# Late modulation of a diffusion layer: four products in four column strips of TensorE

## The reference, cut to what matters

```python
mod = silu(c) @ w_mod + b_mod          # two vectors c; w_mod is 1024 x 6144
shift1, scale1, gate1, shift2, scale2, gate2 = six parts of 1024
h  = x * (1.0 + scale1) + shift1
x  = layer_norm(ALPHA * x + gate1 * mix(h), ln1_g, ln1_b)
h2 = x * (1.0 + scale2) + shift2
x  = layer_norm(ALPHA * x + gate2 * peer(h2), ln2_g, ln2_b)
```

## Time and profile before

| | |
|---|---|
| median of three runs | 3380.88 us |
| the profiled execution | 3382.47 us, of which the span is 3380.5 us |
| TensorE busy, share of the span | 3271.4 us, 97% |
| mean granted clock of TensorE | 0.989 |
| late modulation, L852 from first to last start | 365.4 to 412.5 us |
| first output projection, L895 | from 430.1 us |
| `experts` block, L1673 | from 1220.0 us |

### The profile page before, as it was taken

One profiled execution on the slowest core, in us unless ns is written; L12 is line 12 of the kernel. 1 busy time (PEld: TensorE's weight loads), 2 busy tenths in 40 slices (PEclk: granted clock), 3 DMA queues, 4 the chain that ended last, 5 costly groups with the idle time before them and its releaser, 6 DMA issues.

```text
span 3380.5 us, 46340 instructions
## 1 busy us (share of the span) xinstructions
PE 3271.4 (97%) x17054; PEld 2748.4 (81%) x17054; DVE 2591.1 (77%) x5319; ACT 1237.8 (37%) x2289; POOL 1563.1 (46%) x969
## 2 busy tenths in 40 slices
PE   8999999999998879999999999999999999999997
PEld 3566367787887669998999999998999999999996
DVE  0232137888877879998999888889899998888866
ACT  1232233333332853333333333333333433333333
POOL 1100000688866238888888888432233232222201
PEclk9999999999999989999999999999999999999998
DMA  9600525666667589999999999999998999998943
GB/s 394 256 21 19 226 113 187 188 172 179 168 189 206 203 307 350 344 355 340 350 355 352 367 351 362 382 358 340 361 369 344 367 369 352 357 350 343 352 161 122
DMA packets 290754, 952.91 MB, mean 282 GB/s; under 512 B 92901, under 2 KB 146277, under 8 KB 231784
## 3 DMA queue, kind: packets, MB, share of 16 engines
q1 hardware_dynamic: 154314, 513.36, 41.1%
q0 software_dynamic: 135936, 436.53, 37.6%
q10 hardware_dynamic: 288, 0.16, 0.0%
HBM read 888.70 MB, written 61.24 MB: 281 GB/s over the span
## 4 chain that ended last, share of the span: by engine, by line
PE 52%; DVE 8%; DMA 3%; issue 1%; ACT 1%; SPq 0%; DVEq 0%; ACTq 0%
PE bank L1673 26%; PE bank L1687 26%; DMA work<-in_u 2%; DVE ring L1800 2%; DVE acc L1817 2%; DVE uL L1986 1%; DVE vL L1981 1%; DVE ga L2013 1%; DVE cL L1978 0%; ACT vR L1752 0%; DVE slots L1922 0%; ACT uR L1760 0%; DMA work<-x_scratch 0%; DVE st L1946 0%; DVE slots L1943 0%
## 5 line engine op out<-in xcount | busy, mean ns | idle before, releaser
L1634 POOL DMA_INDIRECT ring<-in_uv,slots x384 | 582.8, 1518 | 794.2 <-DVE carry L1817 684.8
L163 POOL DMA_INDIRECT g_cells<-slots x384 | 704.1, 1834 | 355.7 <-DVE slots L1399 237.2
L1673 PE MATMUL bank<-hR,uR 128*128 128x384 f32 x2048 | 688.8, 336 | 20.2 <-DVE uL L1986 20.2
L1673 PE MATMUL bank<-hR,uL 128*128 128x384 f32 x2048 | 688.7, 336 | 0.0
L1673 PE MATMUL bank<-hL,uR 128*128 128x384 f32 x2048 | 687.2, 336 | 0.0
L1746 ACT ACTIVATE cR<-ga 128x384 fp32r<-128x384 f32 x256 | 134.6, 526 | 953.9 <-PE bank L1687 598.8
L1687 PE MATMUL bank<-vR,cR 128*128 128x512 f32 x1536 | 477.5, 392 | 0.7 <-DVE slots L1922 0.7
L1687 PE MATMUL bank<-vR,cL 128*128 128x512 f32 x1536 | 476.0, 391 | 0.0
L1687 PE MATMUL bank<-vL,cR 128*128 128x512 f32 x1536 | 475.7, 391 | 0.0
L1800 DVE CUSTOM_DVE_ANT_0 ring<-ring,slots 128x1024 f32<-128x1024 f32 x384 | 467.6, 1255 | 0.0
L1673 PEld LDWEIGHTS bank<-hR,uR 128*128 128x128 f32 x2048 | 385.7, 188 | 31.6 <-DVE uL L1986 21.9
(11 more groups left out here) (301 smaller groups left out, 4105.6 us busy)
## 6 DMA issues: line engine op xcount, KB each, us to landing
work<-in_u SPq DMA_DIRECT2D x256, 512.0 KB
work<-in_v SPq DMA_DIRECT2D x256, 512.0 KB
work<-in_w_pq SPq DMA_DIRECT2D x36, 2048.0 KB
work<-in_w_o SPq DMA_DIRECT2D x18, 2048.0 KB
g_cells<-work POOLq DMA_DIRECT2D x32, 768.0 KB, 7.1
work<-g_blocks SPq DMA_DIRECT2D x32, 768.0 KB
work<-g_cells SPq DMA_DIRECT2D x32, 768.0 KB
g_blocks<-big SPq DMA_DIRECT2D x8, 2048.0 KB, 6.3
```

Source lines behind the costliest of these rows:

```text
L163: pool.indirect_dma_start(out=cells_of(g_dram, i), out_offset=bass.IndirectOffsetOnAxis(ap=slots[:, i, D + k:D + k + 1].bitcast(U32), axis=0),
L1634: pool.indirect_dma_start(out=ring[:, k % R, :], out_offset=None, in_=a["uv"], in_offset=bass.IndirectOffsetOnAxis(ap=ids[:, k // P, k % P ...
L1673: mm = pe.matmul(A[t][:, 0:CW], w[:, t, k, :], h[:, k, :], start=(k == 0 and w is uR and h is hR), stop=(k == DK - 1 and w is uL))
```

## The change

The stationary operand becomes `silu_4`: silu padded with zeros to 32 columns, eight blocks, and a ninth block of ones in its first two columns. Product k of a chunk goes into column strip q = k % 4, that is into partitions 32 q to 32 q + 31 of the bank, so that each strip sums two products. The bias is no third row any more: a product with one row (K = 1) of ones by the bias row adds it in strip 0. ScalarE copies all 128 partitions instead of two, and the products of `use` and `second` have 128 rows of `sel_4` (ones where the partition belongs to the row, in all four strips) in place of three, which sums the strips. That holds for `ch` 1 to 5. `ch` 0, 6 and 7 keep the old form. VectorE makes `silu_4` and `sel_4` at the start of `middle`, ahead of its first work on attention. SyncE issues the bias as six DMAs of one row each, ahead of the weights of `ch` 3 and 4; `mod(1)` waits for five of them.

```diff
+        sel_4 = sb(c, "sel4", [P, 2])
+        silu_4 = eq_high[:, 512:512 + (DK + 1) * 32].rearrange("p (k m) -> p k m", m=32)
 def mod_row(ch):
-            if ch < 4:
-                return carry[0:3, ch * 512:(ch + 1) * 512]
-            return eq_high[0:3, (ch - 4) * 512:(ch - 3) * 512] if ch < 6 else mrow[0:3, ch % 2, :]
+            if 0 < ch < 6:
+                return carry[:, (1 + ch % 2) * 512:(2 + ch % 2) * 512]
+            return mrow[0:3, ch % 2, :] if ch else carry[0:3, 0:512]
...
 SyncE, slot 0
+                        sp.dma_start(carry[2:3, 0:512], a["b_row"][0:1, :]).then_inc(row_in[0], 16)
+                        for ch in range(1, 6):
+                            sp.dma_start(bias_row(ch), a["b_row"][ch:ch + 1, :]).then_inc(row_in[1], 16)
                         load("mod", 3)
                         load("mod", 4)
-                        sp.dma_start(carry[2:3, 0:4 * 512]...).then_inc(row_in[0], 16)
-                        sp.dma_start(eq_high[2:3, :]...).then_inc(row_in[1], 16)
...
 mod(ch) on TensorE
+                    if ch == 1:
+                        pe.wait_ge(sel_ready, 2)
+                        pe.wait_ge(row_in[1], 5 * 16)
                     for k in range(DK):
-                        mm = pe.matmul(ps[0:2, :], silu[:, k, :], w[:, k * 512:(k + 1) * 512],
-                                       start=(k == 0), stop=(k == DK - 1))
-                    mm.then_inc(w_mm, 1)
+                        q = k % 4
+                        pe.matmul(ps[32 * q:32 * q + 32, :], silu_4[:, k, :], w[:, k * 512:(k + 1) * 512],
+                                  start=(k < 4), stop=(k > 4))
+                    pe.matmul(ps[0:32, :], silu_4[0:1, DK, :], bias_row(ch), start=False, stop=True).then_inc(w_mm, 1)
...
 row(ch) on ScalarE
-                act.activation(mod_row(ch)[0:2, :], ps[0:2, :], ACT.Copy).then_inc(f, 1)
+                    rows = slice(0, P if ch < 6 else 2)
+                    act.activation(mod_row(ch)[rows, :], ps[rows, :], ACT.Copy).then_inc(f, 1)
...
 VectorE, start of the block
+                ch.step(dve.memset(silu_4[:, :, :], 0.0))
+                dve.tensor_copy(silu_4[:, 0:DK, 0:2], silu[:, :, :])
+                dve.tensor_reduce(sel_4[:, :], ident[:, :].rearrange("p (q m) -> p m q", q=4)[:, 0:2, :], axis=AX.X, op=ALU.add)
+                ch.step(dve.memset(silu_4[:, DK, 0:2], 1.0))
```

More of the change, by code:

```diff
@@ L729, in mod_row, with bias_row @@
         def mod_row(ch):
-            if ch < 4:
-                return carry[0:3, ch * 512:(ch + 1) * 512]
-            return eq_high[0:3, (ch - 4) * 512:(ch - 3) * 512] if ch < 6 else mrow[0:3, ch % 2, :]
+            if 0 < ch < 6:
+                return carry[:, (1 + ch % 2) * 512:(2 + ch % 2) * 512]
+            return mrow[0:3, ch % 2, :] if ch else carry[0:3, 0:512]
+        def bias_row(ch):
+            return eq_high[0:1, 0:512] if ch == 5 else gl[0:1, :, :].rearrange("p m d -> p (m d)")[:, (ch - 1) * 512:ch * 512]
         def emptied(*key):
@@ L863, in gate_part, with sums_of @@
                         mm.then_inc(w_mm, 1)
+                def sums_of(ch, m):
+                    return sel_4[:, m:m + 1].to_broadcast([P, P]) if ch == 1 else sel[:, m:m + 1].to_broadcast([3, P])
                 def use(ch):
@@ L868, in use @@
                         pe.wait_ge(*emptied("mod", ch))
[L869 to L872, removed]
                     if ch == 0:
-                        pe.wait_ge(sel_ready, 1)
+                        pe.wait_ge(row_in[0], 16)
+                    elif ch >= 6:
+                        pe.wait_ge(row_in[ch % 2], 32 if ch == 6 else 6 * 16)
                     if 2 <= ch < 6:
                         for k in range(4):
-                            mm = pe.matmul(ps[:, 2 * k:2 * k + 2], mod_row(ch)[:, k * P:(k + 1) * P], sel[:, :],
+                            mm = pe.matmul(ps[:, 2 * k:2 * k + 2], mod_row(ch)[:, k * P:(k + 1) * P], sel_4[:, :],
                                            start=True, stop=True)
@@ L880, in use @@
                     else:
-                        pe.matmul(ps[:, :], sel[:, 0:1].to_broadcast([3, P]), mod_row(ch),
+                        pe.matmul(ps[:, :], sums_of(ch, 0), mod_row(ch),
                                   start=True, stop=True).then_inc(w_mm, 1)
@@ L885, in second @@
                     ps = bank("use2", ch)
-                    pe.matmul(ps[:, :], sel[:, 1:2].to_broadcast([3, P]), mod_row(ch),
+                    pe.matmul(ps[:, :], sums_of(ch, 1), mod_row(ch),
                               start=True, stop=True).then_inc(w_mm, 1)
@@ L1244, in _ @@
                 ch = Chain(dve, chain)
+                ch.step(dve.memset(silu_4[:, :, :], 0.0))
+                dve.tensor_copy(silu_4[:, 0:DK, 0:2], silu[:, :, :])
+                dve.tensor_reduce(sel_4[:, :], ident[:, :].rearrange("p (q m) -> p m q", q=4)[:, 0:2, :], axis=AX.X, op=ALU.add)
+                ch.step(dve.memset(silu_4[:, DK, 0:2], 1.0))
                 dve.tensor_tensor(sel[:, :], ident[0:3, 0:2], ident[0:3, 2:3].to_broadcast([3, 2]),
-                                  ALU.add).then_inc(sel_ready, 1)
+                                  ALU.add).then_inc(sel_ready, 2)
                 dve.wait_ge(k_ready, 1)
```

## The result

The changed kernel takes 3366.01 us (median of 5 runs, 3362.45 to 3369.52) where the kernel before takes 3385.17 (5 runs, 3380.35 to 3389.01). The ratio is 0.9942, with a 95% interval from 0.9930 to 0.9954: 19.6 us faster (15.6 to 23.7). I had forecast 13.7 us less and 3367.2 us.

The account below looks back on a forecast made before the run. TensorE, busy in 97% of the span, was taken as the bound. Five chunks from 38.8 to 24.6 us, less 0.5 for a later start, gain 13.7: 3380.9 to 3367.2 us; 8-in-10 range 3355 to 3383.

Parts of the forecast that it names:

- the likeliest case: Late chunks: strips overlap in pairs, sixteen passes in 9 steps, 4.92 us a chunk; 3367.2 us in all, chance 0.45.
- chunks do not come near 4.9 us: Failure sign in TensorE's timeline: each late chunk should take about 4.9 us to the next row.
- the window of mod 2 at a clock of 1.00: Sign for the second late chunk: full granted clock, where the profile showed 0.81.
- The strips: Eight products of two passes in a late chunk: 3.86 us, between bounds of 1.72 and 8.16 us.
- four at once: Rival for the late chunks: all four strips overlap, 2.78 us a chunk, 24.4 us gained, 3356.5 us; chance 0.22.
- The bias product: New one-row product at each late chunk's end: 0.86 us uncovered, with total shape changes 0.2 instead of 0.1 us.
- The bias wait: Ahead of and in mod 2: earlier bias DMAs remove 2.2 us of idle and 1.7 us of low clock.
- The clock: In the late chunks: mod 2's 1.7 us low-clock loss goes; one fall of 1.7 us allowed in the range.
- Start of mod 1: First late chunk waits for VectorE and five bias rows: 0.3 to 2.1 us later, 0.5 taken.
- Copies, spreading products, weights: Around the chunks: 128-row copies (0.60 us) and spreading products cost nothing, and later weight DMAs cause no wait.
- Carried to the end: Behind the slots: the full gain carries on, with `experts` starting some 13.7 us earlier than 1220.04.
- the gain given back: Rival behind the slots: shared DMA traffic or waits absorb half of the gain, 3374 us; chance 0.08.

Follow-up runs that it names:

- neighbouring strips: Products 0 and 1 in strip 0, 2 and 3 in strip 1 and so on, otherwise the changed kernel; 3363.35 us, ratio 0.9945 to the kernel before.
- the experiment on it alone: The kernel before with only its two bias DMAs issued ahead of the weights of ch 3 and 4; 3381.68 us, ratio 0.9993.
- with one strip: The changed kernel with all eight products of a late chunk in strip 0 and 32 rows copied; 3389.75 us, ratio 1.0014 to the kernel before.
- the bias in row 127: The changed kernel without bias products, bias rows sent by DMA into partition 127; 3354.81 us, then 3356.26 us in a second measurement.

## Why the prediction was right, and where it was not

The direction and the range hold, but the likeliest case was not what happened. Two errors of opposite sign stood in it, and that the size came near is luck. By its own signs ("I am wrong if chunks do not come near 4.9 us", "the window of mod 2 at a clock of 1.00") it was wrong twice. Of the time itself, 3367.2 against 3366.01 us, the nearness is luck once more: I counted from 3380.88 us, and from the later median of 3385.17 the same sum gives 3371.5. The chances of the cases add up to 0.71 faster, 0.23 the same and 0.06 slower, not 0.70, 0.24 and 0.06; nothing hangs on it.

*What bounds it.* Right. TensorE ends last in these slots, and what its list lost there is found again at the first output projection: from the block's first product to it 67.80 us before, then 49.05, 46.14 and 46.27 us.

*The strips.* This is the step that failed: "product 1's first pass can start only beside product 0's second. So pairs overlap". It argued from rows of one strip to the order among strips. Measured: all four overlap, four steps, 1.86 us to the bias product against the 3.86 + 0.1 forecast. The rival "four at once", given 0.22, has the mechanism: 2.78 us a chunk, measured 2.83. Here the Trainium skill, "TensorE: Matmul & The Clock Gate", section on packing small matmuls, bears both ways, as the prediction said: that matmuls in different column strips run side by side the traces bear out, with 3.76x for four strips (6.99 to 1.86). The sentence there that matmuls start and end in program order can't be taken to mean that a strip's waiting second pass holds back the next strip: strict order in starting gives nine steps in the changed kernel and thirteen with neighbouring strips, and both took four (1.86 and 1.87 us).

*The bias product.* 0.86 + 0.1 forecast, 0.97 measured, uncovered. With it taken away the slots shrank by 9.0 and 6.8 us in the two pairs of traces; 4.85 of each are the five products, the rest is less low clock.

*The bias wait.* Right: the 2.2 us are gone, in both traces of the experiment on it alone the slots are 4.2 us shorter. But the 1.7 us of low clock in mod 2, which I laid to the idle, is not gone in the changed kernel: mod 2 took 3.06, 3.22 and 3.31 us instead of 1.86, without any idle ahead of it.

*The clock.* Not in the sum, beyond one fall in the range. By four at once the slots should have taken 67.8 - 24.4 = 43.4 us, or 43.0 with the start of mod 1 as measured; they took 49.1, 46.1 and 46.3, so 3.1 to 6.1 us went to passes at 1.2 GHz that the sum has at 2.4. The rows bear the sum out: in the first trace 1.6 us in mod 1, 2.1 in mod 2 with its bias product, 2.1 in slot 1 and 0.2 in mod 3. That is the second error. It goes against the first (10.7 us too little for the strips, 24.4 against 13.7), and so the forecast came as near the 19.6 us measured as it did.

*Start of mod 1.* I took 0.5 us later; counted from the block's first product it is 3.22 us against 3.12 (365.43 - 362.31), 0.1. Five DMAs of one row were issued 0.29 us apart and no wait for them is seen.

*Copies, spreading products, weights.* Right: copies 0.60 us, L887 1.05 us with 128 rows as L877 with three, no wait for weights in the changed kernel. One reading was off without harm: w_o leaves in two halves over 9.72 us (395.75), so the second leaves about 25 us ahead of L895 and not 34.4.

*Carried to the end.* As far as can be told, right: `experts` starts at 1202.52 instead of 1220.04 us, 17.5 us earlier. The stretches behind took 3.0 and 1.2 us more in the first trace, 3.3 and 2.3 in the second, 0.9 and 2.8 in the third. The middle took longer with one strip too (793.0 us against 789.9, no gain to give back), and 789.9 with the bias in row 127 and the full gain, but 794.4 in that kernel's other trace. So it is not the gain given back but a spread of some 4 us from trace to trace, which goes with the granted clock of the middle, 0.98 or 0.97. Of the kernel before there is one trace, and it is of the quick group.

## What to carry to other kernels

A product with few columns in its result (here 2 of 128) is worth putting into column strips: four strips were 3.76 times as fast as one, in both orders of the products that were tried, with the two passes of fp32, and a spreading product that was there anyway sums them. Then look at what was added around it: a one-row product over 512 columns costs as much as a full one (0.97 us), and a free partition of a tile that is copied anyway can carry the bias and saves it. And look first what a chunk covers: the same edit won 4 us a chunk in one place and nothing in the other, where the chunk covered VectorE.

## What the runs showed of the hardware that was not expected

Strips queue on their own: four passes in a row for one strip leave the next three free (1.87 us). With one, two and four strips the same work takes 6.99, 3.56 and 1.86 us. A sequence of TensorE products with one and three rows, 2.9 us long, was followed by the low clock in 6 of 6 traces, although TensorE was busy throughout; where this sequence was not there, in none of 6, of which five have no such one-row product. Why stays open, and so does why mod 1 was slow in five of thirteen traces.
